# Every second round of cached key pages transposed by VectorE in 32x32 blocks

## What is computed

```
h = x + 1/2 * norm(swiglu_ffn_1(norm(x)))
p = norm(h) @ w_in            # gated DeltaNet: 4 heads of 128; stick-breaking attention: 8 heads of 64
h = h + norm(concat(o_delta, o_stick) @ w_o)
y = h + 1/2 * norm(swiglu_ffn_2(norm(h)))

# stick-breaking attention of the 8 sequences of 4 queries, over 2048 cached keys and 4 own keys
z = einsum('bqhd,bkhd->bhqk', q, k) * 64 ** -0.5 + bias[h]
log_not = where(mask, log_sigmoid(-z), 0)
between = reverse_cumsum(log_not) - log_not
a = where(mask, exp(log_sigmoid(z) + between), 0)
out = einsum('bhqk,bkhd->bqhd', a, v)
```

## Time and profile before

| | |
|---|---|
| median of the runs | 2364.34 us (2360.7 to 2367.49) |
| time of the profiled execution | 2363.2 us |
| its span in the profile | 2361.5 us |
| mean granted clock of TensorE | 0.988 of full |
| PE busy | 2272.0 us, 96% |
| DVE busy | 1644.3 us, 70% |
| ACT busy | 1057.1 us, 45% |
| `b3` in the profile | from 1211.5 us to about 1506 us |
| key rounds in it | from 1227.9 us to about 1376 us |

### The profile page before, as it was taken

The page is one execution under the profiler, slowest core; times in us unless marked ns, Lnnn a source line. Parts: engine busy times, 40 slices in busy tenths (PEclk is TensorE's granted clock), DMA queues, the critical chain, the costliest instruction groups (busy, mean ns, idle before and its releaser), DMA issues. The chain is left out here.

```text
span 2361.5 us, 47384 instructions
## 1 busy us (share of the span) xinstructions
PE 2272.0 (96%) x18644; PEld 2019.1 (86%) x18644; DVE 1644.3 (70%) x2774; ACT 1057.1 (45%) x1919; POOL 48.9 (2%) x108
## 2 busy tenths in 40 slices
PE   7999999999999999999969999899999999999998
PEld 7999999987879888888858866578999999997786
DVE  7766766656885487677657898657676766655886
ACT  7322222234554667566645555435522323233453
POOL 0000000000000100000010001010000000000000
PEclk9999999999999999999979999899999999999999
DMA  5343333365463233233258878723243432437454
GB/s 161 103 137 117 108 128 102 116 214 187 134 187 108 63 75 69 54 59 74 37 153 294 277 254 310 235 79 118 59 159 102 130 121 87 151 116 237 128 166 153
DMA packets 356274, 328.40 MB, mean 139 GB/s; under 512 B 103929, under 2 KB 264057, under 8 KB 356112
## 3 DMA queue, kind: packets, MB, share of 16 engines
q1 hardware_dynamic: 356112, 326.16, 44.5%
HBM read 254.63 MB, written 71.47 MB: 138 GB/s over the span
## 5 line engine op out<-in xcount | busy, mean ns | idle before, releaser
L1242 PE MATMUL a_q<-a_uh,a_p_hi 128*128 128x352 f32 x672 | 233.6, 348 | 0.6 <-ACT a_xp L1333 0.6
L1244 PE MATMUL a_q<-a_uh,a_p_lo 128*128 128x352 f32 x672 | 216.6, 322 | 0.0
L1243 PE MATMUL a_q<-a_ul,a_p_hi 128*128 128x352 f32 x672 | 216.1, 322 | 0.0
L1242 PEld LDWEIGHTS a_q<-a_uh,a_p_hi 128*128 128x128 f32 x672 | 126.6, 188 | 23.5 <-issue 21.6
L1243 PEld LDWEIGHTS a_q<-a_ul,a_p_hi 128*128 128x128 f32 x672 | 127.1, 189 | 0.1
L1244 PEld LDWEIGHTS a_q<-a_uh,a_p_lo 128*128 128x128 f32 x672 | 126.2, 188 | 0.0
L884 PE MATMUL c_q<-c_b_hi,c_a_hi 128*128 128x512 f32 x264 | 105.4, 399 | 3.9 <-DVE c_a_lo L783 3.0
L884 PE MATMUL a_q<-a_b_hi,a_a_hi 128*128 128x512 f32 x264 | 103.7, 393 | 3.2 <-DVE a_a_lo L783 3.0
L885 PE MATMUL c_q<-c_b_hi,c_a_lo 128*128 128x512 f32 x264 | 104.7, 396 | 0.0
L886 PE MATMUL c_q<-c_b_lo,c_a_hi 128*128 128x512 f32 x264 | 104.6, 396 | 0.0
L886 PE MATMUL a_q<-a_b_lo,a_a_hi 128*128 128x512 f32 x264 | 102.9, 390 | 0.0
(11 more groups left out here) (735 smaller groups left out, 7635.9 us busy)
## 6 DMA issues: line engine op xcount, KB each, us to landing
b_page<-in_cache_k SPq DMA_DIRECT2D x128, 256.0 KB, 4.2
b_page<-in_cache_v SPq DMA_DIRECT2D x128, 256.0 KB, 4.3
a_w_raw<-in_ffn_gu SPq DMA_DIRECT2D x44, 512.0 KB, 5.1
c_w_raw<-in_ffn_gu SPq DMA_DIRECT2D x44, 512.0 KB, 5.0
a_a_raw<-hid_rows SPq DMA_DIRECT2D x66, 256.0 KB, 2.7
c_a_raw<-hid_rows SPq DMA_DIRECT2D x66, 256.0 KB, 2.7
a_p_raw<-in_w_in SPq DMA_DIRECT2D x28, 512.0 KB, 4.2
a_raw_d<-in_ffn_d SPq DMA_DIRECT2D x11, 1024.0 KB, 5.0
```

Source lines behind the costliest of these rows:

```text
L1242: nc.tensor.matmul(self.pm[at % 2][:, 0:TB], wh, self.uh[t][:, c], start=(c == 0), stop=False)
L1243: nc.tensor.matmul(self.pm[at % 2][:, 0:TB], wh, self.ul[t][:, c], start=False, stop=False)
L1244: mm = nc.tensor.matmul(self.pm[at % 2][:, 0:TB], wl, self.uh[t][:, c], start=False, stop=(c == KC - 1))
```

## The change

Even rounds stay as they were up to the copies: PE turns all four pages, and ACT now makes all four copies (L2897 before), where DVE made two of them.

Odd rounds change. Each of the four DMAs puts a whole page in one group of 32 partitions (`page[rows_in(b), slot]`), with four successive tokens, 8 KB of one page, in each partition. DVE waits for the page and transposes it with four instructions of 128x512 in blocks of 32x32 straight into `k_turned[1]`. PE turns nothing. A block then holds, for the four sequences one below the other, 32 of the 512 key values in the partitions, and 32 tokens in the columns. The scores (`block_scores`) again take 16 products with 32 stationary columns and 128 moving ones. The moving columns of one product are read with `t` outside and `s` inside, which steps through memory by 512 elements (2048 bytes) from one column to the next. The stationary queries are in another layout (`q_in`, in memory of `mixed`), with zeros for the other sequences. In even rounds (`natural_scores`) the queries lie in a wider `qb` and the rows of the scores come out in the same order as in odd rounds: pair of heads, sequence, head, query. Masks and the copy to `wt` follow this order. The round of the own keys takes 4 products, where it took 16.

For `q_in` the queries are stored once more in the first part (`q_blocks`, 4 DMAs), and read into 4 groups of 32 partitions (4 DMAs, issued between the loads of the queries and of the new keys). DVE makes 24 small copies for the queries, where it made 16. PE waits for the queries at the first scores, where it waited ahead of all streams. GpSimd (POOL) zeroes two more tiles and makes four more small selections.

```diff
+                if kind == "query":
+                    sp.dma_start(self.q_blocks[:, 4 * hp:4 * hp + 4, :].rearrange("r j n -> j r n"), ring[hp % 2][:, T_P:T]).then_inc(...)
...
+            for b in range(4):
+                sp.dma_start(q_block[rows_in(b)], q_blocks).then_inc(E("q_cols_in"), 16)
...
                         yield key_time(*KEY_ROUNDS[old]) + SP_AT["pages"][0]
-                        sp.wait_ge(E("k_turned1"), 2 * old + 2)
+                        sp.wait_ge(E(f"k_turned{old % 2}"), 4 * (old // 2) + 4)
...
+                        if keys and n % 2 == 1:
+                            sp.dma_start(page[rows_in(b), n % SLOTS].rearrange("p s n -> p (s n)"),
+                                         src.rearrange("g (t s) n -> t (g s n)", s=4)).then_inc(E(f"page_in{n % SLOTS}"), 16)
...
             def turn_keys():
                 for n, (gi, p) in enumerate(KEY_ROUNDS):
-                    for half in range(2):
+                    if n % 2 == 1:
+                        continue
+                    for b in range(4):
...
+                        at = 2 * n + b
+                        at_least(pe, E("k_copied"), at - 2)
+                        for c in range(4):
+                            mm = nc.tensor.transpose(pk[at % 3][:, c], page[:, n % SLOTS, b, c * P:(c + 1) * P], ident[:])
...
+            def block_scores(out, gi, n):
+                keys = k_turned[n % 2].rearrange("p b c n -> p (b c n)").rearrange("p (s j t) -> p j t s", s=4, t=R)
+                for j in range(4):
+                    for c in range(4):
+                        mm = nc.tensor.matmul(out[rows_in(c), 0:P], q_in[:, gi, 4 * c + j], keys[:, 4 * c + j], start=(j == 0), stop=(j == 3))
+                mm.then_inc(E("z_mm"), 1)
...
-            def key_copies():
+            def turn_keys():
                 for n, (gi, p) in enumerate(KEY_ROUNDS):
+                    if n % 2 == 0:
+                        continue
+                    for z in range(4):
+                        yield key_time(gi, p) + DVE_AT["turn_keys"][z // 2]
+                        if z == 0 and n >= 2:
                             dve.wait_ge(E("z_mm"), turned_free(n))
+                        if z == 0:
+                            dve.wait_ge(E(f"page_in{n % SLOTS}"), 64 * (n // SLOTS) + 64)
+                        nc.vector.transpose(k_turned[n % 2][:, z].rearrange("p c n -> p (c n)"), page[:, n % SLOTS, z]).then_inc(E("k_turned1"), 1)
```

More of the change, by code:

```diff
@@ new lines, in natural_scores @@
+            def natural_scores(out, gi, n):
+                for b in range(4):
+                    for c in range(4):
+                        mm = nc.tensor.matmul(out[rows_in(c), 0:P], qb[:, gi, c, rows_in(b)], k_turned[0][:, b, c], start=(b == 0), stop=(b == 3))
+                mm.then_inc(E("z_mm"), 1)
+            def block_scores(out, gi, n):
+                keys = k_turned[n % 2].rearrange("p b c n -> p (b c n)").rearrange("p (s j t) -> p j t s", s=4, t=R)
+                for j in range(4):
+                    for c in range(4):
+                        mm = nc.tensor.matmul(out[rows_in(c), 0:P], q_in[:, gi, 4 * c + j], keys[:, 4 * c + j], start=(j == 0), stop=(j == 3))
+                mm.then_inc(E("z_mm"), 1)
@@ L2735, in products, with own_scores @@
+            def own_scores(out, gi):
                 for c in range(4):
-                    for b in range(4):
-                        mm = nc.tensor.matmul(out[R * b:R * b + R, :], qb[:, gi, c, b], moving(b, c), start=(c == 0), stop=(c == 3))
+                    mm = nc.tensor.matmul(out[rows_in(c), 0:T_S], q_own[:, gi, c], ks[:, c], start=True, stop=True)
                 mm.then_inc(E("z_mm"), 1)
@@ L2743, in scores @@
                     at_least(pe, E("z_out"), r - 1)
-                    if p < PAGES:
-                        for e in range(2):
-                            pe.wait_ge(E(f"k_copied{e}"), 2 * (PAGES * gi + p) + 2)
-                        products(flat(pz[r % 2])[:, 0:P], gi, lambda b, c: k_turned[(PAGES * gi + p) % 2][:, b, c])
-                    else:
-                        products(flat(pz[r % 2])[:, 0:T_S], gi, lambda b, c: ks[:, c])
+                    if r == 0:
+                        pe.wait_ge(E("masks_out"), 1)
+                        pe.wait_ge(E("q_ready"), 1)
+                    n = PAGES * gi + p
+                    if p == PAGES:
+                        own_scores(flat(pz[r % 2]), gi)
+                    elif n % 2 == 0:
+                        pe.wait_ge(E("k_copied"), 2 * n + 4)
+                        natural_scores(flat(pz[r % 2]), gi, n)
+                    else:
+                        pe.wait_ge(E("k_turned1"), 2 * n + 2)
+                        block_scores(flat(pz[r % 2]), gi, n)
             def values():
@@ L2891, in key_copies @@
                 for n, (gi, p) in enumerate(KEY_ROUNDS):
-                    for half in range(2):
-                        yield key_time(gi, p) + ACT_AT["key_copies"][half]
-                        if half == 0 and n >= 2:
+                    if n % 2 == 1:
+                        continue
+                    for b in range(4):
+                        yield key_time(gi, p) + ACT_AT["key_copies"][b // 2]
+                        if b == 0 and n >= 2:
                             act.wait_ge(E("z_mm"), turned_free(n))
-                        act.wait_ge(E("k_turned0"), 2 * n + half + 1)
-                        nc.scalar.activation(k_turned[n % 2][:, 2 * half], pk[(4 * n + 2 * half) % 3][:], ACT.Copy).then_inc(E("k_copied0"), 1)
+                        act.wait_ge(E("k_turned0"), 2 * n + b + 1)
+                        nc.scalar.activation(k_turned[0][:, b], pk[(2 * n + b) % 3][:], ACT.Copy).then_inc(E("k_copied"), 1)
             def weigh():
@@ L3203, in _ @@
             dve.wait_ge(E("zeros_made"), 1)
-            interleave(chain(), advance(), gates(), norms(), prepare(), key_copies(), logits(), weigh(), keep(), finish())
+            interleave(chain(), advance(), gates(), norms(), prepare(), turn_keys(), logits(), weigh(), keep(), finish())
 KEPT = "rk rkb rq rqg rkbg rkd beta g big_g".split()
```

93 lines of the change are left out of this document (48 added, 45 removed).

## The result

The changed kernel takes 2386.69 us, the median of four runs (2381.89 to 2391.3), against 2364.04 of before on the same chip: a ratio of 1.0095, with a 95% interval of 1.0067 to 1.0124. It is slower by 22.6 us; the forecast was 2356 with a range up to 2378. The profiled execution took 2390.06 us.

What follows compares the result with a forecast made beforehand. PE was taken as the bound, DVE and transfers close behind. From the profiled 2363.2 us, -10 and -8 (stretches), +5 (uncovered steps), +4.7 (start) gave 2354.9; with 1.1 for the median, 2356 us, range 2338 to 2378.

Steps and rivals of the forecast that it cites:

- Who is late next: Key rounds' two halves (stretches): transfers end last in the first, losing 10 us; DVE in the second, losing 8.
- Rival 3: Odd rounds' loads: pages in 32 partitions move 1.47 times slower, +1.4 us a round; 2367 us, chance 0.17.
- Rival 4: Odd scores: four strided streams take turns, up to 3.06 us more a round; 2387 us, chance 0.13.
- The strided read: Odd scores' moving columns 2048 bytes apart: taken as 0, upper bound 49 us.
- rival 2: Odd scores: strided read costs four times a contiguous one, 0.84 us more a round; 2363 us, chance 0.20.
- The start: Start of `b3`: 24 query copies for 16 and four more DMAs add 4.7 us, bounds 2.4 and 6.
- DVE's transposes: Odd key rounds: 64 transposes of 128x512 at 0.71 us replace 64 copies at 684 ns, nearly nothing either way.
- ACT's four copies: Even key rounds: four copies of 598 ns, instead of two in every round; same total, counted as nothing.
- uncovered steps: Key rounds: `invert` steps whose gaps turned pages no longer fill, four places, 5 us, ends 2 and 13.
- The -18 of the two stretches: Key rounds' two halves: 10 and 8 us saved, of the 32 us of turns taken off PE.

Runs made afterwards that it cites:

- e4: Kernel before, with each page of odd rounds loaded into one block of 32 partitions, PE still turning it: 2388.54 us, 1.0098.
- e2: Changed kernel with odd pages loaded over 128 partitions, as even ones are (wrong keys under odd scores): 2365.59 us, 1.0006.
- e8: e1 with the odd rounds' pages of sequences 2 and 3 issued by ACT, the others by SP: 2382.61 us, 1.0089.
- e15: e1 with each narrow load cut in two, each half taking every second of 32 partitions, sequences in order 0, 2, 0, 2, 1, 3, 1, 3: 2377.48 us, 1.0051.
- e1: Changed kernel with the odd scores reading contiguous columns and DVE putting the logits in order: 2386.82 us, 1.0100.
- e3: Changed kernel with both odd pages loaded over 128 partitions (wrong keys) and contiguous reads of odd scores: 2357.61 us, 0.9979.
- e6: Kernel before, with odd pages in 8 KB pieces in 32 partitions each, four apart: 2364.46 us, 0.9995.
- e14: e1 with each narrow load cut in two halves of 16 adjacent partitions, sequences in order 0, 2, 0, 2, 1, 3, 1, 3: 2384.56 us, 1.0076.

## Why the prediction was wrong

**The step that failed** is in "Who is late next": "The same pages must pass, so the transfers end last, and the stretch can lose about 10 us." The transfers were named as the bound, at 58.7 us of 69, and given the same need for pages that now go to blocks of 32 partitions. That need is 2.5 to 3.0 us more in each odd round. With eight odd rounds in the first stretch the need is 79 to 83 us where the forecast had 58.7, and over all key rounds 58.7 + 62.4 + 16 x 2.5 to 3.0 = 161 to 169 us of the 177.9 that they took. The view over the key rounds as a whole agrees: a share of 0.92 of 177.9 us, 164 us, where the kernel before had 0.82 of 148.4, 122 us. e4 shows this cause by itself (23 us slower), and e2 shows the change without it (1.0006).

**Rival 3** was this mechanism. It took 1.47 times, +1.4 us a round, from one load of 192 KB; the measured factor is 2. That factor hung on one load, of whose 2.8 us all but 1.1 were latency by the same rows. Its other half, that transfers at 70 us would only eat the gain, followed from the small price. I wrote that two loads to each half could hide it; in the order 0, 1, 2, 3 they don't. Where a version brought the landings down (e8, e15), PE waited for ACT, which had part of the issues, or for pages that SP issued late.

**Rival 4** gave 2387, which is what was measured, by a mechanism that did not happen: the score line is 2.20 us and not 4.08, and e1, without the stride, is as slow. The number was a coincidence.

**The strided read** was priced 0 "because the nearest row has room". It costs 1.12 us in each odd round (2.20 for 1.08), rival 2's mechanism with more than its 0.84. The rate of a contiguous stream did not carry over to a strided one. The Trainium skill's rule of the 16-byte line (SBUF — State Buffer, Door 1: The DMA port swizzle) pointed the right way; the runs show a doubling for this one step of 2048 bytes, and no other step was tried. In the changed kernel it adds nothing that shows; beside wide loads 8 us.

**The start** was put at 4.7 us, with 2.4 as its lower bound; the first turned page came 1.2 later (2.8 in e3). One pair of executions says little here: the first turned page lies between 1225.7 and 1228.8 us in the five profiled kernels that start as before, and between 1228.1 and 1231.5 in the thirteen that start as the changed one, 2.4 us later in the mean. Of this 1.3 us is there already when DVE's first copy starts, so the four more DMAs cost less than the 2 us of the sum but were not hidden. In the changed kernel that copy starts at 1217.31, where it started at 1217.13, and the last of the 24 ended at 1223.11:

```profile
1217.31 0.21 DVE L3235 COPY b_qb<-b_run 64x64 f32<-64x64 f32 x1 [5.92 <-DMA b_run<-q_blocks]
...
1222.25 0.86 DVE L3240 COPY w_mixed<-b_run 32x32 f32<-32x32 f32 x4
```

The 24 copies took 5.8 us, 0.24 each, not 0.304.

**DVE's transposes** were forecast at 0.71 us and took 0.677, so 64 of them cost what 64 copies had. ACT's four copies cost next to nothing, as said: in the changed kernel PE waited for them once, 0.8 us ahead of the first scores. The **uncovered steps**, put at 5 us: PE waited 4.1 us for L3110 in the changed kernel and 3.7 in e3, where it waited 0.8 for L3073 before, inside the 2 to 13.

```profile
PE b_D L2660 <- DVE b_x L3110: 4.1, 2, 2.8
```

**The -18 of the two stretches** was too large as well, which the failed step hid. e3 has wide loads and contiguous reads, what the forecast assumed, and its 2357.6 agrees with the 2356. That is luck in good part: its key rounds are shorter by 5.4 us where the sum had 13, and its start later by 2.8 where it had 4.7, so they end 2.6 us sooner and not 8.3. The first product behind `b3` comes 2.0 us sooner (1509.76 for 1511.71); the other 5.9 us of the shorter span lie behind it, where the work is the same. I had taken each stretch down to its next bound at 95 to 100% of one engine. In a static order with three partners no engine reached that: DVE stood at 85%.

## What to carry to other kernels

Before a load's shape is changed, price it by where its partitions lie and not by its bytes: look at the DMA share and the GB/s of the stretch together, and where a stretch has a share of 0.85, expect a longer load to end last. A saving on the busiest engine is worth only what the next resource and the static order leave of it, here some 3 to 5 of 32 us, hardly clear of noise, and an idle PE also lost clock. When two faults lie on one path, undo each by itself and both together, and put each alone into the kernel before: one run of the changed kernel would have blamed the strided read, whose line had doubled and which cost nothing that shows there.

## What the runs showed of the hardware

- A load of 256 KB to one block of 32 partitions costs the DMA engines twice a load to 128 (3.0 us on 2.9 in a round of four; packets of 8 KB at 595 ns for 309); to 32 partitions four apart it costs nothing more (e6, 0.9995), and 2 KB or 8 KB packets make no difference (1.0102, 1.0098).
- Narrow loads hold back the wide ones behind them on the same queue: those of even rounds landed in 8.9 us in the median in the changed kernel, where pages took 4.2 before. Loads of 16 partitions: adjacent ones landed in 7.7 us, every second one of 32 in 4.5.
- The issue of a load that names every second partition takes SP longer: eight of them 5.9 us in the mean in e15, for 4.2 of adjacent ones in e14.
- A float32 product of 32 stationary and 128 moving columns whose moving columns lie 2048 bytes apart takes 427 ns in the mean, for 276 with contiguous columns; a group of 32 such instructions takes 2.2 us for 1.08.
- DVE's 32x32 block transpose of 128x512 float32 takes 677 ns, as long as its copy of that size from PSUM, 684.
